# Moving the last layer's condition vectors of a two-block network from TensorE in the attention to VectorE in the feed-forward

## The reference, cut to what matters

```
def ada_mod(cond, w, b):
    m = jax.nn.silu(cond) @ w + b            # w: 1024 x 6144
    return jnp.split(m[..., None, :], 6, axis=-1)

for layer in range(2):
    sh1, sc1, g1, sh2, sc2, g2 = ada_mod(c, ada_w[layer], ada_b[layer])
    xn = rms_norm_2(h, norm_mix_g[layer]) * (1 + sc1) + sh1
    y = attention_and_fourier(xn, ...) if layer == 0 else pool_mix(xn, ...)
    h = h + g1 * y
    hn = rms_norm_2(h, norm_ffn_g[layer]) * (1 + sc2) + sh2
    h = h + g2 * ((silu(hn @ w1[layer]) * (hn @ w3[layer])) @ w2[layer])   # hidden width 2816
```

## Time and profile before

| | |
|---|---|
| median of 3 runs | 1718.15 us (1711.32 to 1720.84) |
| the profiled execution, its own time | 1718.55 us |
| its span | 1716.5 us |
| share of the span: PE, DVE, ACT | 80%, 38%, 10% |
| TensorE's mean granted clock | 0.90 |
| HBM read | 586.58 MB |

### The profile page before, as it was taken

The page is one execution under the profiler, slowest core; times in us unless marked ns, Lnnn a source line. Parts: engine busy times, 40 slices in busy tenths (PEclk is TensorE's granted clock), DMA queues, the critical chain, the costliest instruction groups (busy, mean ns, idle before and its releaser), DMA issues.

```text
span 1716.5 us, 24774 instructions
## 1 busy us (share of the span) xinstructions
PE 1375.1 (80%) x10737; PEld 857.7 (50%) x10737; DVE 655.6 (38%) x1116; ACT 163.1 (10%) x413; POOL 5.0 (0%) x10
## 2 busy tenths in 40 slices
PE   6898998676667756675776667667999999999997
PEld 4797854222212212221222122215777999999997
DVE  2647553501100101110011001106547777877775
ACT  2013320100000000000000000001422000120001
POOL 1000000000000000000000000000000000000000
PEclk8998999988888878878888888889999999999999
DMA  9989959999999999999999999997953654524541
GB/s 402 365 329 420 424 209 400 405 431 431 432 431 431 431 431 432 431 431 431 431 432 431 431 431 431 432 430 303 414 245 122 234 197 170 217 89 160 208 181 64
DMA packets 46847, 590.16 MB, mean 344 GB/s; under 512 B 5392, under 2 KB 7856, under 8 KB 9664
## 3 DMA queue, kind: packets, MB, share of 16 engines
q1 hardware_dynamic: 43184, 583.89, 81.7%
q10 hardware_dynamic: 3600, 5.34, 1.0%
HBM read 586.58 MB, written 2.62 MB: 343 GB/s over the span
## 4 chain that ended last, share of the span: by engine, by line
DMA 50%; PE 44%; DVE 4%; ACT 1%; issue 1%; SPq 0%; DVEq 0%; ACTq 0%
DMA ring<-in_w 45%; PE ps L2064 5%; PE ps L2059 4%; PE ps L2060 4%; PE ps L1574 4%; PE ps L1865 3%; PE ps L1753 3%; PE ps L1512 3%; PE ps L1886 3%; PE ps L2075 2%; PE ps L2074 2%; PE ps L2073 2%; DMA ring<-in_w_in 2%; DMA ring<-in_w_ada 2%; DVE ring_parts L823 1%
## 5 line engine op out<-in xcount | busy, mean ns | idle before, releaser
L1865 PE MATMUL ps<-ring,mixT 128*32 128x512 f32 x2016 | 297.3, 725 | 164.7 <-DMA ring<-in_w 163.7
L1886 PE MATMUL ps<-ring,arena 128*32 128x512 f32 x1024 | 171.9, 807 | 108.2 <-DMA ring<-in_w 98.1
L1865 PEld LDWEIGHTS ps<-ring,mixT 128*32 128x32 f32 x2016 | 61.6, 121 | 374.1 <-issue 192.5
L1199 DVE TENSOR_TENSOR arena<-arena,ps 128x512 f32<-128x512 f32 x16 | 11.0, 687 | 487.9 <-PE ps L1865 487.9
L823 DVE TENSOR_TENSOR ring_parts<-ring,ring_parts 128x1024 fp32r<-128x1024 f32 (+3 forms) x119 | 189.7, 1625 | 1.1
L2059 PE MATMUL ps<-mixT_parts,ring_parts 128*128 128x256 f32 x704 | 169.5, 281 | 0.6 <-issue 0.6
L2060 PE MATMUL ps<-mixT_parts,ring_parts 128*128 128x256 f32 x704 | 169.5, 281 | 0.0
L1886 PEld LDWEIGHTS ps<-ring,arena 128*32 128x32 f32 x1024 | 33.0, 130 | 230.0 <-DMA ring<-in_w 147.1
L820 DVE CAST ring_parts<-ring 128x1024 fp32r<-128x1024 f32 (+3 forms) x119 | 100.4, 890 | 122.4 <-DMA ring<-in_f 72.8
L2059 PEld LDWEIGHTS ps<-mixT_parts,ring_parts 128*128 128x128 f32 x704 | 133.2, 189 | 2.1 <-issue 1.4
L2060 PEld LDWEIGHTS ps<-mixT_parts,ring_parts 128*128 128x128 f32 x704 | 132.8, 189 | 0.8
(11 more groups left out here) (380 smaller groups left out, 1389.7 us busy)
## 6 DMA issues: line engine op xcount, KB each, us to landing
ring<-in_w SPq DMA_DIRECT2D x190, 2048.0 KB, 25.8
ring<-in_ada_w SPq DMA_DIRECT2D x24, 2048.0 KB, 13.5
ring<-in_f SPq DMA_DIRECT2D x22, 2048.0 KB, 7.8
ring<-in_w_ada SPq DMA_DIRECT2D x12, 2048.0 KB, 14.4
ring<-in_f SPq DMA_DIRECT2D x22, 1024.0 KB, 6.7
ring<-in_w_in SPq DMA_DIRECT2D x5, 2048.0 KB, 18.2
ring<-in_w_out SPq DMA_DIRECT2D x2, 2048.0 KB, 13.3
ring<-in_mix_in SPq DMA_DIRECT2D x2, 2048.0 KB, 21.1
```

The lines of the kernel that those rows point to most:

```text
L1865: last = mm(ps[rows[u], j, :], XeT[:, 2 * m + k, rows[u]], w[:, u, k * FE:(k + 1) * FE], start=(m == 0 and k == 0), stop=(m == 3 and k == 1))
L1886: last = mm(ps[rows[u], m, :], heT[:, k, rows[u]], w[:, u, m * 512:(m + 1) * 512], start=(k == 0), stop=(k == FE // P - 1))
```

## The change

- Chunks of layer 0: 4 of the 12 stay in the first block's attention (the columns that the context needs, and shift and scale of the mixer), the other 8 move to the second block's attention.
- The 12 chunks of layer 1 leave the ring. Their matrix comes transposed (`adaT`, 12 blocks of two halves of 1 MB), and VectorE makes the sums in the feed-forward: `ada_blocks` multiplies 1024 columns by `crow`, the condition vector on every partition, and sums them (`scalar_tensor_tensor` with `accum_out`), four such operations for a block of 512 outputs. Ten blocks lie in layer 0's steps 0 to 9, one in layer 1's step 0, one in its step 9. The sums come out as columns, so `columns` is not needed for them, and the gates are spread with `gate_columns` (8 products of 128 columns).
- SyncE loads the halves (`ada_load`) behind each step's `w13` and `w2` of layer 0; each half waits until VectorE has used the half before it (`ad_used`).
- The high parts of steps 1 to 21 are made by ScalarE (`high_pieces`: 4 pieces of 1024 columns for `w13`, 2 for `w2`), ahead of the step's silu; VectorE makes the low parts as before, each quarter once its high piece is there.
- `crow` is made after the context's projection: 8 products on TensorE, one copy of 1024 columns on ScalarE, for which TensorE waits before it goes on to quad 1.

```diff
@@ SyncE
-            for c in range(12):
+            for c in range(4):
                 load(RL0 + c, A["ada_w_2"][c], CHUNK)
...
-            for c in range(1, 12):
-                load(RL1 + c, A["ada_w_2"][12 + c], CHUNK)
+            for c in range(1, 8):
+                load(RL1 + c, A["ada_w_2"][4 + c], CHUNK)
...
+            def ada_load(d, i=None):
+                for h in range(2):
+                    if d:
+                        before = 2 * (d - 1) + h + 1
+                        sp.wait_ge(ad_used, before if i is None else i * 4 + before)
+                    else:
+                        sp.wait_ge(*((side_used, 2), (b_T, 8))[h])
...
+                    sp.dma_start(halves[h], src).then_inc(ad_in[h], 16)
...
                 sp.dma_start(w2[s], part(A["f2"])).then_inc(w2_in[s], 16)
+                if l == 0:
+                    ada_load(c, i)
+                elif c == 2:
+                    ada_load(NF)
@@ ScalarE
+            act.wait_ge(cx_tr, 3)
+            nc.scalar.activation(crow, ps[:, 2:4, :].rearrange("p b n -> p (b n)"), ACT.Copy).then_inc(cx_T, 1)
...
                 for f in range(2):
+                    if more and f == 0:
+                        high_pieces(w13H[s], w13[s], 4, (w13_in[s], at), w13_high)
+                    elif more:
+                        high_pieces(w2H[s], w2[s], 2, (w2_in[s], at), w2_high)
@@ VectorE
+            def ada_blocks(d, i, blocks, into):
+                for b in blocks:
+                    h, at = b // 2, 16 * (d + 1)
+                    if b % 2 == 0:
+                        dve.wait_ge(ad_in[h], at if i is None else i * 32 + at)
+                    v = piece(halves[h], b % 2)
+                    last = stt(v, v, 1.0, crow, ALU.mult, ALU.mult,
+                               accum_out=acc[:, into + b:into + b + 1])
+                    if b % 2:
+                        last.then_inc(ad_used, 1)
...
             def ffn_step(l, c, i=None, more=True):
+                ada = c < NF - 1 and (l == 0 or c in (0, NF - 2)) 
+                if ada:
+                    ada_blocks(d, i, (0, 1), into)
                 if more:
-                    split13(g + 1, i, (0, 1))
+                    low13(g + 1, i, (0, 1))
+                if ada:
+                    ada_blocks(d, i, (2,), into)
                 hidden(g, 0, i)
                 if more:
-                    split13(g + 1, i, (2, 3))
-                    split2_high(g + 1, i)
+                    low13(g + 1, i, (2, 3))
+                if ada:
+                    ada_blocks(d, i, (3,), into)
                 hidden(g, 1, i)
                 if more:
-                    split2_low(g + 1)
+                    low2(g + 1, i)
@@ TensorE
-            for u, (a, b, c) in enumerate((((2,), (), (3,)), ((4,), (5,), (6,)), ((7,), (8,), (9,)), ((10,), (11,), ()))):
+            for u in range(PAIRS):
...
             pe.wait_ge(cx_T, 2)
+            for k in range(KD):
+                last = mm(ps[:, 2 + k // 4, (k % 4) * P:(k % 4 + 1) * P], cond[:, 1, k, 0:1].to_broadcast([P, P]), ident,
+                          start=True, stop=True)
+            last.then_inc(cx_tr, 1)
+            pe.wait_ge(cx_T, 3)
             with pe.Fori(0, E // QD - 2) as i:
...
-                   2: (lambda: ada(4), lambda: ada(5)), 3: (lambda: mixed(0), lambda: ada(6)),
-                   4: (lambda: ada(7), lambda: mixed(1)), 5: (lambda: ada(8), lambda: (ada(9), mixed(2))),
-                   6: (lambda: ada(10), lambda: mixed(3)), 7: (lambda: ada(11), lambda: None)}
+                   2: (lambda: ada(4), nothing), 3: (lambda: mixed(0), nothing), 4: (lambda: ada(5), lambda: mixed(1)),
+                   5: (lambda: mixed(2), nothing), 6: (lambda: ada(6), lambda: mixed(3)), 7: (lambda: ada(7), nothing)}
```

More of the change, by code:

```diff
@@ L779, in ffn @@
                 ffn_step(l, 0)
-                with act.Fori(0, (NF - 1) // 2) as i:
+                rounds = (NF - 1) // 2 - l
+                with act.Fori(0, rounds) as i:
                     for c in (1, 2):
                         ffn_step(l, c, i)
+                for c in range(2 * rounds + 1, NF):
+                    ffn_step(l, c, None, c < NF - 1)
+                    if c == NF - 2:
+                        gate(6, 0)
             gate(3, 2)
@@ L1069, in _ @@
             probabilities(3)
[L1070 removed]
+            ada_first()
             combined(3)
             columns(0, 4, 8, 0, 2)
[L1073 removed]
+            columns(1, 0, 4, 2, 3)
             dve.wait_ge(a_done, PAIRS)
@@ L1397, in _ @@
                 combined2(n)
-            columns(2, 0, 8, 2, 4)
+            columns(2, 4, 8, 2, 4)
+            dve.wait_ge(col_ev, 4)
             modulation(modcol[:, 1, 16:32], V("nffn0"))
[L1401 to L1407, removed]
-                        last = high(q(w13H[s], n), q(w13[s], n))
-                    link(last)
+            piece = lambda v, n: v[:, n * 1024:(n + 1) * 1024]
@@ L1410, in split13, with low13 @@
+            def low13(g, i, quarters):
+                s = g % 2
                 for n in quarters:
-                    last = low(q(w13L[s], n), q(w13[s], n), q(w13H[s], n))
+                    if g:
+                        dve.wait_ge(w13_high, 4 * (g - 1) + n + 1 if i is None else i * 8 + (4 * (g - 1) + n + 1))
+                    last = low(piece(w13L[s], n), piece(w13[s], n), piece(w13H[s], n))
                 if 3 in quarters:
                     last.then_inc(w13_split, 1)
-            def split2_high(g, i):
-                s, at = g % 2, 16 * (g // 2 + 1)
-                dve.wait_ge(w2_in[s], at if i is None else i * 16 + at)
-                link(high(w2H[s], w2[s]))
@@ new lines, in ada_biases @@
+            def ada_biases(a, b):
+                dve.wait_ge(ad_used, b // 2)
+                tt(acc[:, a:b], acc[:, a:b], CB("ada1")[:, a:b], ALU.add).then_inc(ad_cols, 1)
+            done(dve, RMO - 2)
+            dve.wait_ge(w13_in[0], 16)
+            for n in range(4):
+                last = high(piece(w13H[0], n), piece(w13[0], n))
+            link(last)
+            low13(0, None, range(4))
+            dve.wait_ge(w2_in[0], 16)
+            link(high(w2H[0], w2[0]))
+            low2(0, None)
```

138 lines of the change are left out of this document (75 added, 63 removed).

## The result

The changed kernel takes 1746.17 us (median of 4 runs, 1742.56 to 1747.19), the kernel before 1717.64 (4 runs, 1711.32 to 1720.84): a ratio of 1.0167, 95% interval 1.0134 to 1.0200. It is slower by 28.5 us. The profiled execution took 1746.72 us, with a span of 1744.9.

The account below looks back on a forecast made before the run. TensorE with its partners' latency bounds the first attention, DMA the experts, TensorE layer 0's feed-forward. Terms -9.9 + 2.9 - 3.5 + 31 + 1.8 + 1.0 = +23.3 on 1718.55 give 1742 us; range 1722 to 1768.

Parts of the forecast that it names:

- The feed-forward, the loop: Layer 0's steps: `w13` waits behind the `adaT` half and fourth sum, 19.7 us against TensorE's 16.74; +31 us.
- the residual's +1.8: End of layer 0: VectorE finishes some 2.5 us later, 0.7 of it already counted; +1.8 us.
- the part of the gate that lies there (-0.8): Gap ahead of layer 1: the gate's work leaves it; -0.8 us.
- The casts: Feed-forward steps: high-part casts moved to ScalarE cost nothing, as it idles over 5 us ahead of each silu.
- The sums: Feed-forward, VectorE: each sum of 1024 columns takes 1.22 us; a separate read-out could add 0.2.
- Rival 2: Feed-forward: the sums run at half rate, 2.36 us each, loop 21.9 us, kernel 1767 us; chance 0.07.
- The first attention: First attention with 8 chunks fewer on TensorE: -9.9 us, between 5 and 16 gained.
- the forecast's own signs of being wrong: Layer 0 steps of 16.7 us or `w13` not behind `adaT`; sums of 2.3 us; an attention no shorter.
- that bound (5): First attention's smallest gain, 5 us: TensorE idles more in the pairs, with two more stretches at half speed.
- `crow`: Ahead of quad 1: TensorE waits for eight products and a ScalarE copy, so the experts' stream restarts later; +2.9 us.
- The second attention: Second attention, 12 chunks become 8: -3.5 us, between 1.5 and 8 gained.
- Layer 1 and the gate: Layer 1: its steps lose 0, the gate moves into its last steps; +1.8 us.

Follow-up runs that it names:

- sums_ahead: Changed kernel with VectorE making all four sums of a step at its start, instead of two, one and one: 1720.96 us, ratio to before 1.0019.
- highs_back: Changed kernel with the high-part casts returned from ScalarE to VectorE, which keeps the sums: 1781.13 us.
- few_bytes: Changed kernel with the adaT halves after the first pair cut to an eighth of their columns: 1732.20 us.
- short_sums: Changed kernel with each sum made over 64 of its 1024 columns: 1736.73 us.
- highs_alone: Kernel before the change with only the high-part casts moved to ScalarE: 1716.20 us, ratio to before 0.9998.
- ahead_row: Changed kernel with all four sums at the step's start and `crow` made ahead of layer 0's feed-forward: 1717.02 us, ratio to before 1.0006.
- row_later: Changed kernel with `crow` made ahead of layer 0's feed-forward, in place of three filler matmuls: 1745.22 us, ratio to before 1.0161.
- chunks_in_pair: Changed kernel with the condition chunk ahead of the first queries moved into pair 0: 1745.85 us, ratio to before 1.0163.
- ahead_row_chunks: Changed kernel with sums at the step's start, `crow` ahead of layer 0's feed-forward and two chunks in pair 0: 1715.51 us, ratio to before 0.9999.

## Why the prediction held, and where its sizes were off

- **The feed-forward, the loop.** +31 us forecast, and with the residual's +1.8 and the part of the gate that lies there (-0.8) 32.0 up to layer 1's start; measured 28.9 (-1.6 to +27.3). The step is 19.3 for 19.7. In the step shown, which is 19.1, `w13` behind the half was counted at 10.1 and is 0.88 + 8.91 = 9.8, and the hand-overs come to 0.2 rather than 0.4. The step with the pooling loads is 25.4 us (1343.41 to 1368.85) for 24.7. sums_ahead shows that the cause is the order, and highs_back, few_bytes and short_sums that it closes as a loop. The 2.4 us that I gave the half came out at 2.2 for the two together: `w13` is issued 0.9 behind it and its bytes are then 1.3 later than in few_bytes.
- **The casts.** "Cost nothing" held (highs_alone). Inside the loop they even help: VectorE in ScalarE's place makes it 2.5 us longer (highs_back).
- **The sums.** 1.22 us each was the value taken and is the value measured (L1455, 1024 columns of two fp32 tensors in SBUF, accumulated), with a read-out of 0.08 that costs nothing beside it (the third sum's read-out and the next instruction both start at 1440.30, 1.15 us behind the sum's start). Rival 2 is out. By the rule weighed there, of the Trainium skill, page Vector Engine (DVE) Microarchitecture Reference, section Points that are easy to get wrong, the prediction's estimate was 2.36 us; the measurement decides against it for this form.
- **The first attention.** The step that failed in size: -9.9 forecast, -4.1 at project_out and -3.4 at the experts in this pair of profiles, and less than that if all are taken. project_out starts at 216.0 in the profile before, but at 211.4 in highs_alone, which has the same order up to there; in the eight profiles with the changed order it starts at 211.0 to 218.1, 213.7 on average, as the two of the old order do. So no gain of the stage can be told; two profiles of the old order are few, but ahead_row's twelve runs say the same of both attentions together. And an attention no shorter with eight chunks gone was one of the forecast's own signs of being wrong. In the pair of profiles the terms are these. Up to scores 1 it gave more than I took: -2.4 for -1.5 at scores 0, -2.5 for -0.5 from there to scores 1. The term for scores 1 to 2 was -2.7 and came out at +3.5, since TensorE ran there at half clock; I had named that bound (5) and not taken it, and the result is below it. The -2.3 of scores 2 to 3 held exactly (14.0 to 11.7). The -2.05 and -0.8 behind it came to -0.4, again at half clock; the profile before ran at 0.63 and 0.51 from 208 to 216 itself, and highs_alone, at 1.00 there, takes 18.3 us for 21.4, so that against it this stretch is 2.8 longer after the change.
- **`crow`.** 2.9 forecast, 3.3 measured at quad 1 (-3.4 to -0.1) and 4.4 at the end of the experts (+1.0), as row_later's profile has it with 4.3. The products and the copy are as costed. The further 1.1 us don't go with `crow`: from quad 1 to the end of the experts sums_ahead, which has it in the same place, takes 862.7 us as the kernel before does, and the changed kernel 863.9. Where they come from is open.
- **The second attention.** -3.5 forecast, -2.7 measured (128.6 us for 131.3, from the norm's transposes behind the experts to those ahead of the feed-forward). It scatters too: in the seven profiles with this order and `crow` in its old place it takes 128.6 to 131.4 us, in the two of the old order 131.3 and 132.1. **Layer 1 and the gate.** +1.8 forecast, +1.1 measured; its steps don't wait.

The sum was +23.3 and the execution's difference is +28.2: errors of 6.5, 1.5 and 0.8 us upward (first attention, `crow`, second attention) against 3.1 and 0.7 downward (layer 0, layer 1). That 1742 came so near 1746 is in part luck: the loop was counted too long and the front too short.

## What to carry to other kernels

When a queue works in order, a transfer that waits for a late consumer holds every transfer behind it: walk the cycle from an issue round to the same issue again and compare it with the bound engine's step, since shares of busy time (66% DMA, 68% VectorE here) don't show it. The cure costs nothing if the consumer can go early: free the buffer before the next important issue is due. And work taken off TensorE in a latency-bound stretch need not be worth its duration: here eight chunks fewer went with a fall of the granted clock in all eight profiles and no gain that can be told. So read the clock in windows of a few us, before and after, and not as the mean of a stage, and read a stage in more than one execution before a difference of a few us is put down to the change.

## What the hardware showed that I had not expected

- The granted clock fell to its lower level behind waits of 0.66 to 1.36 us in pair 0, for some 12 us (164 to 176), in which TensorE was busy throughout; the seven other kernels with this order of work show the same from 164 to 172. The order does not always settle it: two executions with another order in common (chunks_in_pair, ahead_row_chunks) had it at 1.00 and at 0.50 in 168 to 172.
- A transfer of 1.05 MB ahead of one of 2.1 MB in the same queue cost it nearly its whole time at the full rate, counted from its own issue: ScalarE starts 9.6 to 9.9 us behind the issue of the half in most steps, whether `w13` is issued 0.5 or 0.9 us after it, against 7.6 behind the issue of `w13` with an eighth of the bytes ahead.
- Twelve small products in each of three pairs went with a stop of 3.86 us, without any data waited for, 1000 us later, and with 8 us on the kernel's time; one profile shows the stop, and that the one causes the other is not shown.
- A VectorE instruction that accumulates is followed by a read-out of its own, 0.08 us on the sums, and the next instruction starts together with it where it waits for nothing else.
